# A two-block transformer kernel: x and context as two sequences with their own weight passes, and adaLN on TensorE

## The reference

```python
for i in range(DEPTH):
    m = adaln(c, ada_w[i], ada_b[i])[:, None]
    mc = adaln(c_ctx, ada_w[i], ada_b[i])[None]
    h = half_ffn(h, m, 0, g[0], g[1], ffn_w_in[i, 0], ffn_w_out[i, 0])
    hc = half_ffn(hc, mc, 0, g[0], g[1], ffn_w_in[i, 0], ffn_w_out[i, 0])
    # layer 0: differential attention; layer 1: grouped-query attention
    # x attends over context and x, the context over itself
    # then the residual and a second half_ffn; in the last layer for x alone
```

## Time and profile before

| | |
|---|---|
| median of 3 runs | 2817.33 us (2813.98 to 2820.81) |
| span of the profiled execution | 2814.7 us |
| TensorE busy | 2602.5 us (92%) |
| VectorE busy | 1710.1 us (61%) |
| ScalarE busy | 1002.3 us (36%) |
| mean granted TensorE clock | 0.928 of full |
| moved by DMA | 351.5 MB |

### The profile page before, as it was taken

How to read it: one execution, slowest core, us unless ns; L and a number is a source line. 1 busy time by engine, 2 the same in 40 slices (tenths; PEclk the granted TensorE clock), 3 DMA queues, 4 the chain that set the end, 5 groups by cost and what they waited for, 6 DMA issues and landing times. The chain is left out here.

```text
span 2814.7 us, 39425 instructions
## 1 busy us (share of the span) xinstructions
PE 2602.5 (92%) x14572; PEld 2247.8 (80%) x14572; DVE 1710.1 (61%) x3265; ACT 1002.3 (36%) x1597; POOL 0.8 (0%) x5
## 2 busy tenths in 40 slices
PE   7989988888998999999987899999899999888997
PEld 7989978758997888877855678888688888667997
DVE  3365554446556888435666678873678863656555
ACT  4244442334443222233255332223322223335443
POOL 0000000000000000000000000000000000000000
PEclk9599997758999999998998999999899999989999
DMA  5245452103543554332310135533245532211443
GB/s 212 106 144 185 157 223 84 43 1 134 180 160 131 180 179 150 110 114 88 113 53 1 60 125 176 178 130 103 80 165 179 179 117 92 94 60 61 165 166 118
DMA packets 65732, 351.54 MB, mean 125 GB/s; under 512 B 7376, under 2 KB 10960, under 8 KB 40528
## 3 DMA queue, kind: packets, MB, share of 16 engines
q1 hardware_dynamic: 62272, 341.86, 34.6%
q10 hardware_dynamic: 3344, 8.12, 0.8%
HBM read 348.91 MB, written 1.05 MB: 124 GB/s over the span
## 5 line engine op out<-in xcount | busy, mean ns | idle before, releaser
L309 DVE TENSOR_TENSOR wlo<-raw,whi 128x2048 fp32r<-128x2048 f32 (+1 forms) x282 | 582.2, 2064 | 602.8 <-ACT whi L302 602.0
L314 PE MATMUL bank<-HN_hi,whi 128*128 128x256 f32 (+1 forms) x2976 | 645.1, 342 | 58.7 <-ACT HN_hi L826 31.8
L302 ACT ACTIVATE whi<-raw 128x2048 fp32r<-128x2048 f32 (+1 forms) x282 | 488.7, 1733 | 526.5 <-PE bank L314 508.3
L314 PE MATMUL bank<-HN_hi,wlo 128*128 128x256 f32 (+1 forms) x2976 | 626.6, 335 | 0.0
L314 PE MATMUL bank<-HN_lo,whi 128*128 128x256 f32 (+1 forms) x2976 | 606.3, 334 | 0.0
L314 PEld LDWEIGHTS bank<-HN_hi,whi 128*128 128x128 f32 x2976 | 485.3, 195 | 137.5 <-issue 33.7
L314 PEld LDWEIGHTS bank<-HN_hi,wlo 128*128 128x128 f32 x2976 | 485.6, 194 | 52.5 <-issue 0.5
L314 PEld LDWEIGHTS bank<-HN_lo,whi 128*128 128x128 f32 x2976 | 479.4, 194 | 53.9
L314 PE MATMUL bank<-G_hi,whi 128*128 128x256 f32 (+1 forms) x1056 | 207.4, 345 | 4.4 <-DVE wlo L309 4.4
L314 PE MATMUL bank<-G_lo,whi 128*128 128x256 f32 (+1 forms) x1056 | 198.9, 336 | 0.0
L314 PE MATMUL bank<-G_hi,wlo 128*128 128x256 f32 (+1 forms) x1056 | 198.6, 336 | 0.0
(11 more groups left out here) (223 smaller groups left out, 2086.5 us busy)
## 6 DMA issues: line engine op xcount, KB each, us to landing
raw<-w_main SPq DMA_DIRECT2D x186, 1024.0 KB, 4.8
raw<-w_down SPq DMA_DIRECT2D x96, 704.0 KB, 4.1
half<-w_ada SPq DMA_DIRECT2D x128, 512.0 KB, 4.4
raw<-w_ada SPq DMA_DIRECT2D x8, 1024.0 KB, 4.7
ARENA<-cmp_k_w ACTq DMA_DIRECT2D x1, 2048.0 KB, 11.4
ARENA<-cmp_v_w ACTq DMA_DIRECT2D x1, 2048.0 KB, 18.6
H<-x SPq DMA_DIRECT2D x1, 1024.0 KB, 6.7
H<-x ACTq DMA_DIRECT2D x1, 1024.0 KB, 6.1
```

The source lines that it names most:

```text
L302: NS.activation(WHI[n % 2][:, 0:size], RAW[slot][:, 0:size], ACT.Copy).then_inc(sems["w_hi"], 1)
L309: NV.tensor_tensor(WLO[slot][:, 0:size], RAW[slot][:, 0:size], WHI[n % 2][:, 0:size].bitcast(fp32), SUB)\
L314: return NT.matmul(out[:, 0:N], (WHI[n % 2], WLO[n % SLOTS])[w][:, k * wk + col:k * wk + col + P], x[xp][:, kx, 0:N], start=start, stop=stop)
```

## The change

x and the context become two sequences of 256 columns, each with buffers, semaphores and banks of its own (`Lane`). Each makes its own passes over the weights: the same weight block is loaded and split once for x and once more for the context. x keeps its whole FFN hidden layer; the context does an FFN in three chunks of hidden tiles (8, 8, 6), and adds the parts of the output up on VectorE. All loads, x's, the context's, those of adaLN and of the compression weights, go through one ring of four raw buffers in the order in which they are taken.

The sequences are generators, whose emission a scheduler interleaves. `x_sequence` leads. Where it yields "L" with a number of microseconds, `fill` emits context half blocks (24 matmuls) or adaLN blocks up to a credit; where it yields "D" (before a dense block) or "d" (in its middle), `pace` emits a short context step, an adaLN block at every second "D" (at every one at first) and, from the third FFN on, up to two context half blocks a block of x. The context starts its first FFN as soon as x has passed its first norm. `need` and `want` emit the adaLN or context steps that x is about to read. Context post-processing is emitted one block late (`lag`).

adaLN runs on TensorE: the two silu vectors, padded to 32 columns, are the stationary operand, the raw weight block moves with 256 columns, and the eight matmuls of a block go to four column positions of the array. ScalarE copies the rows out, two matmuls by a `pick` matrix sum and turn them, and VectorE adds the bias. `gemv_half` and its buffers go. silu is made of a tanh on ScalarE and one more operation on VectorE, for two tiles at a time. Down blocks are now 1024 (or 768) rows by 256 outputs. The high parts have three buffers.

```diff
...
-GEMV, PER_PAIR = {8: 20, 10: 4, 12: 20, 14: 20}, {8: 2, 10: 1, 12: 2, 14: 2}
...
+SLOTS, HIS = 4, 3
...
-        HN = [sb("HN_hi", [P, KD, T2], f32r), sb("HN_lo", [P, KD, T2], f32r)]
-        Y = sb("Y", [P, KD, T2])
-        HALVES = [sb("half0", [P, 2 * T2]), sb("half1", [P, 2 * T2])]
...
+        HX, HC = sb("HX", [P, KD, T]), sb("HC", [P, KD, T])
+        WHI = [sb(f"whi{s}", [P, BLK], f32r) for s in range(HIS)]
...
+        X = Lane("x", 0, HX, HNX, YX, GX, TMPX, SQX, DIAGX[:, :], *(s[:, :] for s in SUMX), 0,
+                 (BANK[2], BANK[3], BANK[0], BANK[1]), (BANK[0], BANK[1]), (BANK[3], BANK[4]), BANK[2], BANK[3], False, False)
+        C = Lane("c", 1, HC, HNC, YC, GC, TMPC, SQC, TMPC[1][:, 0:T], *(s[:, :] for s in SUMC), 64,
+                 None, (BANK[6], BANK[7]), (BANK[7], BANK[6]), BANK[7], BANK[6], True, True)
...
-            def gemv_half(i, t, h, gemv, base):
...
-            def gemv_reduce(i, t, gemv, base):
...
+            def load_weights():
+                for n, (array, index, size, _) in enumerate(plan):
+                    if n >= SLOTS:
+                        sp.wait_ge(sems["block_done"], n - SLOTS + 1)
+                    src = A[array][index[0]][:, index[1]:index[1] + size] if isinstance(index, tuple) else A[array][index]
+                    sp.dma_start(RAW[n % SLOTS][:, 0:size], src).then_inc(sems[f"w_in{n % SLOTS}"], 16)
+
+            def splits(n):
+
+                while split_at[0] < len(mains) and mains[split_at[0]] <= n + 2 \
+                        and (split_at[0] < HIS or mains[split_at[0] - HIS] <= n - 1):
+                    q, m = split_at[0], mains[split_at[0]]
+                    if act:
+                        act.wait_ge(sems[f"w_in{m % SLOTS}"], 16 * (m // SLOTS + 1))
+                        if q >= HIS:
+                            act.wait_ge(*done(mains[q - HIS]))
+                        size = plan[m][2]
+                        NS.activation(WHI[q % HIS][:, 0:size], RAW[m % SLOTS][:, 0:size], ACT.Copy).then_inc(sems["w_hi"], 1)
+                    split_at[0] += 1
+                while split_at[1] < split_at[0] and mains[split_at[1]] <= n + 1:
+                    q, m = split_at[1], mains[split_at[1]]
+                    if dve:
+                        dve.wait_ge(sems["w_hi"], q + 1)
+                        size = plan[m][2]
+                        NV.tensor_tensor(WLO[m % SLOTS][:, 0:size], RAW[m % SLOTS][:, 0:size],
+                                         WHI[q % HIS][:, 0:size].bitcast(fp32), SUB).then_inc(sems["w_lo"], 1)
...
+            def two_tiles(S, n, dsts, x, ks, start, stop, waits=None, signal=None, tiles=2):
+                landed(n)
+                for m in range(tiles):
+                    mm = three(dsts[m], n, m * P, x, ks, start, stop, None if m else waits)
+                    if mm is not None and m == 0 and signal is not None:
+                        mm.then_inc(signal.sem, 1)
+                    if m == 0:
+                        splits(n)
+                    if m == 0 and tiles == 2:
+                        opened[0] = S.tag
+                        yield ("d",)
+                    opened[0] = None
+                if mm is not None:
+                    mm.then_inc(sems["block_done"], 1)
+
+            def after(S, job):
+                if not S.lag:
+                    return job()
+                last, jobs[S.tag] = jobs.get(S.tag), job
+                if last:
+                    last()
+
...
+                    yield ("L", 3.0)
+                    tot_y = add_up(S, S.YY, sum_y, 0, now(f"{t}_sq_sum"), *ready)
...
+                        add_up(S, S.GG, sum_h, 0, now(f"{t}_gg_sum"))
...
+                    yield ("L", 1.5)
+                    rs_y = spread_in(S.DIAG, S.wide_y, diag)
...
+            def modulation():
+                bank = BANK[5]
+                picked = None
+                for b in range(72):
+                    yield ("D",)
+                    n = take("a", "w_ada", b, BLK, False)
+                    landed(n)
+                    if on(pe, silu_c if b == 0 else None, free.get(bank.name)):
+                        for k in range(KD):
+                            g = k % 4
+                            mm = NT.matmul(bank[32 * g:32 * g + 32, 0:T], CCOL[:, k, :], RAW[n % SLOTS][:, k * T:(k + 1) * T],
+                                           start=k < 4, stop=k >= 4, skip_group_check=True, tile_position=(0, 32 * g))
+                        mm.then_inc(sems["block_done"], 1)
+                    splits(n)
+                    rows = up("act_step")
+                    if on(act, done(n), picked):
+                        NS.activation(ROWS[:, :], bank[:, 0:T], ACT.Copy).then_inc(rows.sem, 1)
+                    yield ("L", 0.5)
+                    picked, kept = up("pe_step"), up("ada_out")
+                    if on(pe, rows):
+                        for m in range(2):
+                            mm = NT.matmul(bank[:, T + 2 * m:T + 2 * m + 2], ROWS[:, m * P:(m + 1) * P], vec("pick"), start=True, stop=True)
+                        mm.then_inc(picked.sem, 1)
+                    if on(dve, picked):
+                        NV.tensor_tensor(MOD[:, 2 * b:2 * b + 2, :], bank[:, T:T + 4].rearrange("p (a s) -> p a s", s=2),
+                                         vec("ada_b")[:, 2 * b:2 * b + 2].unsqueeze(2).to_broadcast([P, 2, 2]), ADD).then_inc(kept.sem, 1)
...
+            def need(L, *rows):
+                while any((L, row) not in gains_known for row in rows):
+                    step("a")
+                return [gains_known[L, row] for row in rows]
...
+            def fill(us):
+                credit[0] = min(credit[0] + us, 6.0)
+                late = set()
+                if ahead["c"] == "W":
+                    step("c")
+                while credit[0] > 0:
+                    if ahead["c"] in ("D", "d"):
+                        credit[0] -= 2.9
+                        step("c")
+                    elif ahead["c"] == "L" and "c" not in late:
+                        late.add("c")
+                        credit[0] -= 0.3
+                        step("c")
+                    elif "a" not in paused and ahead["a"] == "D":
+                        credit[0] -= 1.2
+                        step("a")
+                    elif "a" not in paused and ahead["a"] == "L" and "a" not in late:
+                        late.add("a")
+                        step("a")
+                    else:
+                        return
+
+            def pace(kind):
+
+                if ahead["c"] == "W":
+                    step("c")
+                if kind == "D":
+                    spent[0] += 1
+                    if ahead["a"] == "L":
+                        step("a")
+                    if ahead["a"] == "D" and "a" not in paused and ((0, 1) not in gains_known or spent[0] % 2 == 0):
+                        step("a")
+                    for _ in range(urge[0]):
+                        if ahead["c"] in ("D", "d"):
+                            step("c")
+                if ahead["c"] == "L":
+                    step("c")
+                elif kind == "d" and ahead["a"] == "L":
+                    step("a")
+
+            def want(label):
+                while label not in passed:
+                    step("c")
...
+                urge[0] = 2
+                free["x", "gain"] = need(0, 2)
+                yield from ffn(X, 2, post(X, 0, 0), x)
...
+                want("kv0")
+                hold_bank()
...
 def down_blocks(w):
-    return w.reshape(2, HALF, P, KD, P).transpose(3, 0, 2, 1, 4).reshape(-1, P, DBLK)
+    return w.reshape(KF, P, 4, 256).transpose(2, 1, 0, 3).reshape(4, P, KF * 256)
...
```

2468 lines of the change are left out of this document (1243 added, 1225 removed).

## The result

The changed kernel takes 3136.45 us (median of 4 runs, 3133.88 to 3137.02), the kernel before 2815.65 us on the same chip (2811.65 to 2820.81): a ratio of 1.1145, 95% interval 1.1122 to 1.1168. It is 11% slower, where 3% faster was forecast, and lies outside the range.

The account below looks back on a forecast made before the run. TensorE was taken as the bound: 2424 us of full-clock work plus 390 us starved or slowed by the chain through VectorE and ScalarE. 75 + 34 + 12 - 204 = -83 us on 2817 gave 2734 us, range 2660 to 2855.

Parts of the forecast that it names:

- 75 + 34 = 109: TensorE work: +75 us for 512-column matmuls split into two of 256, +34 us net for adaLN moved to TensorE.
- rival 3: adaLN blocks: column tiles run one after another, 276 us instead of 115, giving 2895 us; chance 0.11.
- I price it at nothing: Context's extra weight loads and splits hide behind three blocks of matmuls; beside an adaLN block, 13 us cover 9.0; cost nothing.
- starve the ring beyond the start: Weight ring: adaLN block loads starving it past the start was named as something that would make the prediction wrong; no size.
- so 204 us come back: x's norms and attentions: context and adaLN blocks fill TensorE's waits, recovering 204 of 390 us lost to idle and clock.
- 186 us: Loss expected to remain over all nine stretches after filling: 16, 14, 8, 24, 12, 9, 20, 13 and 70 us.
- 12 for coupling: Shared in-order queues: x's splits and silu wait behind context instructions, 1 us in each of 12 down blocks, +12 us.
- 24 was the forecast: Odd mixer: loss left after filling, 24 of 93 us, its clock loss going nearly whole.
- the tail: Last attention and its norms: 70 of 77 us loss stays, since context work and adaLN are used up earlier.
- by their load (12 us): Even mixer: twelve adaLN blocks demanded at once, each 2.6 us to load against 1.6 us of matmuls, costing 12 us.
- Rival 2: VectorE queue beside x's dense layers: 120 context blocks each delay x's split or silu; 2818 to 2876 us; chance 0.15.
- Rival 4: Context runs out of step, waiting in its own chain where x waits; half the recovery lost, 2836 us; chance 0.07.

Follow-up runs that it names:

- e1_low_look: The changed kernel with the low split's look-ahead counted in main blocks instead of ring positions; 2967.13 us.
- e2_both_look: e1_low_look with the high split's look-ahead counted in main blocks too, up to three ring positions ahead; 3025.88 us.
- e6_spaced: e1_low_look with ready low splits issued ahead of each norm's elementwise chain, and short context steps kept apart from the end of their block; 2943.63 us.
- e13_x_alone: e6_spaced with the whole context lane left out (its keys and values are zeros), x and adaLN kept; 2147.58 us.
- e18_settled: e6_spaced, context started later, 1.5 times fill credit, kept context job ahead of x's norm chain, no context step before x's first block; 2906.68 us.
- e14_no_attn: e6_spaced without the context's norms after its first and without the context's attention; 2835.45 us.
- e15_pool: e6_spaced with the context's low splits on GpSimd instead of VectorE; 3005.86 us.

## Why the prediction was wrong

The change's work was sized rightly. TensorE's work grew by 97 us; the prediction had 75 + 34 = 109 for matmuls. Dense matmuls cost 0.120 us, adaLN 119 us of work (115), so rival 3 (column tiles one after another) is out: a block takes 1.00 us from its start to that of the next matmul. Its rows in e1_low_look, where nothing waits:

```profile
1046.73 0.28 PE L226 MATMUL bank<-HNX_hi,wlo 128*128 128x256 f32 x1
1046.85 0.28 PE L226 MATMUL bank<-HNX_lo,whi 128*128 128x256 f32 x1
1047.06 1.07 PE L959 MATMUL bank<-raw,CCOL 128*32 128x256 f32 x16
...
1048.06 0.39 PE L226 MATMUL bank<-HNX_hi,whi 128*128 128x256 f32 x1
```

Two steps failed, and they make up the miss of 402 us: 169 is what e1_low_look gave back, and 233 is what it leaves over 2734.

*First, "I price it at nothing".* The prediction compared the cover of a block (13 us with an adaLN block among the three) with load and splits (9.0 us). That count of capacity was right and beside the point. What mattered was the place at which a split is issued: look-ahead was counted in ring positions, and the position after the block was spent on an adaLN block. The prediction named adaLN blocks that "starve the ring beyond the start" as what would make it wrong. The place was right, but it is the queue in front of the split that starves TensorE and not the ring (e1_low_look; e2_both_look shows that asking earlier for the load makes it worse). The code for it stood in the diff, and a walk through one x, x, adaLN sequence on each engine's queue would have shown it.

*Second, "so 204 us come back".* With the look-ahead mended the loss is 426, against 369 before. The prediction took x's waits as fixed holes, into which a lane without waits is poured, and left 186 us. 57 up in place of 192 down (204 less 12 for coupling) are 249 us, and the work came out 14 below the forecast (95 against 109), which is the 233 within 2 us. It was right in kind where the context runs only blocks beside x's small matmuls (odd mixer: 107 to 47; 24 was the forecast). By stretch, e6_spaced against the 186: the differential attention and FFN 2 to 4 lose 182 us where 42 were forecast, the start and the even mixer 97 where 30 were, the odd mixer with FFN 0 and 1 71 where 44 were, and the tail 53 where 70 were (the forecast's windows end a little earlier than the layers). Two things were left out for the first of these. The context's own norms and attention make holes as well, which x had shared while both went through one norm of 512 columns. And x's first block behind a hole stands in TensorE's queue behind the context's block that was put in it. The prediction had this as coupling at +12 us for "each of 12 down blocks", so it looked in the wrong place: dense blocks beside dense blocks cost nothing (0.3 us idle in 2000 to 2250), and the norms and the differential attention cost 110 us over x alone in four layers. In the even mixer the prediction priced the adaLN blocks that `need` asks for by their load (12 us); what TensorE waits for there is VectorE, which frees their one bank late (22 us in e6_spaced, 14 of them in one wait), and adaLN costs 29 us of loss there. Rival 2 (coupling takes the place of the waits) named the mechanism, but its place was "the VectorE queue beside x's dense layers", and there it did not happen. Rival 4 said half of the recovery; none of it came. (Rival 2's upper end is 2878, not 2876: 120 x 1.2 us on 2734.)

It also left unsaid that splitting two lanes makes ScalarE change functions more often. Loads of its tables in the changed kernel, and in the kernel before (the two largest groups of each):

```profile
L482 ACT ACT_TABLE_LOAD x21 | 26.9, 1283 | 0.7
L403 ACT ACT_TABLE_LOAD x14 | 18.0, 1283 | 0.2
```

```profile
L538 ACT ACT_TABLE_LOAD x6 | 7.7, 1283 | 0.1
L595 ACT ACT_TABLE_LOAD x6 | 7.7, 1283 | 8.2 <-DVE GA L489 8.1
```

In all they are 51 and 25, at 1.28 us (x alone, e13_x_alone: 27; e6_spaced: 47); those of the root (L482) lie in the norms' chains. What they cost the span was not tried by itself.

Left open: 364 us of loss in e18_settled are 23 more than those of x alone, and x alone loses 341 us with adaLN and 299 without it, not far from the 369 of the kernel before. The waits of x in the last attention do not fill at all because the context's work is used up by then (in e6_spaced the last matmul that reads the context's normed input starts at 2561, and x's last attention follows its norm of 2563), as forecast with 70 us for the tail. How much of FFN 2's 38 us is the context's attention and how much its blocks' evacuations was not separated (e14_no_attn still has 43).

## What to carry to other kernels

When entries of a new kind enter a ring that a look-ahead counts in positions, count what the look-ahead still reaches for the entries that need it; walk one period through each in-order queue, and ask what stands in front of each issued operation, not only whether the time suffices. A second lane poured into the first one's waits has waits of its own: before trusting the filling, price the first lane alone plus the second lane's work; here even that sum was 62 us too low. Measure by leaving a lane out: it gives the account in one number. And give work that runs beside others a buffer to spare: one shared bank ties it to whatever stands in front of the operation that frees it.

## What the runs showed of the hardware that was not expected

- After a wait of 2.70 us TensorE ran on at 0.12 us a matmul from 960.66 for 1.1 us and only then for 3.7 us at 0.21. Behind the same wait at 907.67 the matmuls went at 0.21 us from the first on. So the low clock can follow a wait at once or late, and its cost lies in the block behind the wait.
- Filling waits with 752 unread matmuls of 128 columns did not keep the clock up: low-clock time 143 us against 120.
- Entering and leaving column tiles cost little. The matmul before the adaLN block in e1_low_look starts 0.21 us ahead of it (0.12 otherwise), and the block's sixteen instructions and the way back take 1.00 us, where a quarter of 16 x 0.213 is 0.85. The two differences, 0.09 and 0.15 us, make an estimate of 0.24 us for both changes. The Trainium skill (TensorEngine Tiling (Array Packing), Key Properties) states that a change of tiling mode drains the engine; by this, the trace agrees as far as it goes, with a gap of that size and no row for a drain by itself.
- Beside dense TensorE work at 2.4 GHz, weights came in at 239 to 243 GB/s, and TensorE did not wait for them (in e1_low_look from 250 to 450 it is idle for 0.25 us in all).
- Three VectorE operations with two inputs that ran beside a subtraction on GpSimd ended only 0.3 to 0.6 us behind it, one of them after 3.76 us in place of 0.69 (e15_pool).
